# Small prologue loads moved from SyncE's to ScalarE's DMA queue in a two-block transformer kernel

## What is computed

```python
mod = jax.nn.silu(c) @ w_mod[l] + b_mod[l]
shift, scale, gate = jnp.split(mod, 3, axis=-1)
mod_c = jax.nn.silu(c_ctx) @ w_mod[l] + b_mod[l]
u = rms_norm(h, norm_w[l]) * (1.0 + scale[:, None, :]) + shift[:, None, :]
uc = rms_norm(hc, norm_w[l]) * (1.0 + scale_c) + shift_c
p = u @ w_in[l]
q, k, v = qk_heads(p, q_norm_w[l], k_norm_w[l])
q = rope_2d(q, angles)
```

## Time and profile before

| | us |
|---|---|
| median of 3 runs | 1993.04 (1991.38 to 1993.1) |
| profiled execution | 1991.96 |
| its span, first to last instruction | 1990.3 |
| PE busy | 1774.3 |
| DVE busy | 943.5 |
| ACT busy | 654.2 |
| POOL busy | 521.7 |
| mean DMA rate over the span | 94 GB/s |

### The profile page before, as it was taken

The page is one execution under the profiler, slowest core; times in us unless marked ns, Lnnn a source line. Parts: engine busy times, 40 slices in busy tenths (PEclk is TensorE's granted clock), DMA queues, the critical chain, the costliest instruction groups (busy, mean ns, idle before and its releaser), DMA issues.

```text
span 1990.3 us, 24899 instructions
## 1 busy us (share of the span) xinstructions
PE 1774.3 (89%) x10049; PEld 1484.2 (75%) x10049; DVE 943.5 (47%) x1232; ACT 654.2 (33%) x933; POOL 521.7 (26%) x441
## 2 busy tenths in 40 slices
PE   4997599778697789989999999899677999999997
PEld 3796499568695677668888777799566678888875
DVE  1568577675477764453333222533564343233223
ACT  4312255421223334242322212421564243333113
POOL 0005700344744000358878200078000000000000
PEclk8898799889898889999999999999878999999999
DMA  8453300134522000335556222222100212323321
GB/s 279 156 166 106 106 1 1 66 120 146 180 79 83 1 1 1 127 102 179 194 181 191 92 86 98 65 85 86 42 1 1 85 64 90 100 86 99 101 74 42
DMA packets 154445, 187.22 MB, mean 94 GB/s; under 512 B 6765, under 2 KB 121813, under 8 KB 154356
## 3 DMA queue, kind: packets, MB, share of 16 engines
q1 hardware_dynamic: 154356, 185.96, 29.0%
HBM read 183.85 MB, written 2.10 MB: 93 GB/s over the span
## 4 chain that ended last, share of the span: by engine, by line
PE 61%; POOL 15%; issue 8%; DVE 8%; ACT 5%; DMA 3%; POOLq 0%; SPq 0%; DVEq 0%; ACTq 0%
PE ps L694 7%; PE ps L695 7%; PE ps L696 7%; POOL msum L536 5%; POOL mraw L529 5%; PE ps L712 4%; PE ps L714 4%; PE ps L715 4%; PE ps L1044 4%; PE ps L1045 4%; PE ps L1046 4%; PE ps L788 2%; DMA mfirst<-in_w_mod_dram 1%; DMA mraw<-in_w_mod_dram 1%; PE ps L1017 1%
## 5 line engine op out<-in xcount | busy, mean ns | idle before, releaser
L1044 PE MATMUL ps<-uH,whi 128*128 128x512 f32 x704 | 277.6, 394 | 11.0 <-DVE uL L1581 11.0
L1565 DVE TENSOR_TENSOR wlo<-wraw,whi 128x2048 fp32r<-128x2048 f32 x71 | 176.5, 2487 | 218.8 <-ACT whi L1175 218.6
L1046 PE MATMUL ps<-uH,wlo 128*128 128x512 f32 x704 | 275.6, 392 | 0.0
L1045 PE MATMUL ps<-uL,whi 128*128 128x512 f32 x704 | 275.6, 391 | 0.0
L1175 ACT ACTIVATE whi<-wraw 128x2048 fp32r<-128x2048 f32 x71 | 135.7, 1911 | 346.8 <-PE ps L696 327.9
L712 PE MATMUL ps<-whi,uH 128*128 128x256 f32 (+1 forms) x800 | 230.8, 289 | 11.2 <-DVE uL L1581 11.2
L529 POOL TENSOR_TENSOR mraw<-mraw,cpad 128x1024 f32<-128x1024 f32 x64 | 128.4, 2007 | 398.9 <-PE ps L635 256.6
L714 PE MATMUL ps<-wlo,uH 128*128 128x256 f32 (+1 forms) x800 | 229.4, 287 | 0.0
L715 PE MATMUL ps<-whi,uL 128*128 128x256 f32 (+1 forms) x800 | 229.1, 286 | 0.0
L712 PEld LDWEIGHTS ps<-whi,uH 128*128 128x128 f32 x800 | 157.2, 196 | 12.8 <-issue 12.7
L1044 PEld LDWEIGHTS ps<-uH,whi 128*128 128x128 f32 x704 | 133.2, 189 | 41.1 <-issue 10.8
(11 more groups left out here) (389 smaller groups left out, 3200.6 us busy)
## 6 DMA issues: line engine op xcount, KB each, us to landing
mraw<-in_w_mod_dram SPq DMA_DIRECT2D x104, 512.0 KB, 3.9
wraw<-in_w_gate_dram SPq DMA_DIRECT2D x22, 1024.0 KB, 5.3
wraw<-in_w_up_dram SPq DMA_DIRECT2D x22, 1024.0 KB, 5.5
wraw<-in_w_down_dram SPq DMA_DIRECT2D x16, 1024.0 KB, 5.1
wraw<-in_w_in_odd_dram SPq DMA_DIRECT2D x12, 1024.0 KB, 5.1
wraw<-in_w_in_dram SPq DMA_DIRECT2D x11, 1024.0 KB, 5.4
wraw<-in_w_in_even_dram SPq DMA_DIRECT2D x9, 1024.0 KB, 6.5
mfirst<-in_w_mod_dram SPq DMA_DIRECT2D x16, 512.0 KB, 7.3
```

Source lines behind the costliest of these rows:

```text
L1044: mm(o, h_, uH[:, k], start=(k == 0), stop=False)
L1045: mm(o, h_, uL[:, k], start=False, stop=False)
L1046: last = mm(o, l_, uH[:, k], start=False, stop=(k == KT - 1))
L1565: V.tensor_tensor(wlo[:, n % 2, :], wraw[:, n % 2, :], whi[:, n % 2, :].bitcast(F32), ALU.subtract).then_inc(lo_done, 1)
```

## The change

The same 24 loads, with the same semaphores, are issued by ScalarE ahead of its first wait, in the same order (fifteen vectors, nine tables). SyncE's program begins with tick 0, and its tables between tick 15 and chunk 1 are gone. No load, no size and no wait is changed otherwise.

```diff
@@ SyncE
-            row = lambda ap: ap.rearrange("(r f) -> r f", f=P)
-            for r, ap in ((VC, t["c"][0]), (VCC, t["c_ctx"]), (VC2, t["c_2"][0]), (VBM, t["b_mod"][0]),
-                          (VNW, t["norm_w"][0]), (VCB, t["conv_b"][0]), (VLW, t["conv_ln_w"][0]),
-                          (VLB, t["conv_ln_b"][0]), (VBP, t["b_pw"][0])):
-                v = row(ap)
-                sp.dma_start(vr1[r:r + v.shape[0], 0], v).then_inc(vec_in, 16)
-            sp.dma_start(vr1[0:NV2, 1], t["b_mod_2"].rearrange("l (r f) -> (l r) f", f=P)).then_inc(vec_in, 16)
-            for r, name in ((0, "ln_mix_g_2"), (16, "ln_mix_b_2"), (32, "ln_ffn_g_2"), (48, "ln_ffn_b_2")):
-                sp.dma_start(vr1[r:r + 16, 2], t[name].rearrange("l (r f) -> (l r) f", f=P)).then_inc(vec_in, 16)
-            sp.dma_start(cwr[0:TAPS, :], t["conv_w"][0]).then_inc(vec_in, 16)
             for kp in range(4):
                 load_tick(0, kp)
...
                 if g == 3:
-                    sp.dma_start(ropet[:, 0], t["cos1"].rearrange("(t p) n -> p t n", p=P)).then_inc(tab_in, 16)
-                    sp.dma_start(ropet[:, 1], t["sin1"].rearrange("(t p) n -> p t n", p=P)).then_inc(tab_in, 16)
-                    sp.dma_start(qkw[:, 0], t["q_norm_w"].to_broadcast([P, HD])).then_inc(tab_in, 16)
-                    for tt in range(TT):
-                        sp.dma_start(posi[:, tt:tt + 1], t["positions_2"][0, tt * P:tt * P + P]
-                                     .rearrange("(p o) -> p o", o=1)).then_inc(tab_in, 16)
-                    sp.dma_start(ifr[:, :], t["inv2"].to_broadcast([P, 32])).then_inc(tab_in, 16)
-                    sp.dma_start(qkw[:, 1], t["k_norm_w"].to_broadcast([P, HD])).then_inc(tab_in, 16)
                     load_chunk(1)
@@ ScalarE, ahead of its first wait
+            row = lambda ap: ap.rearrange("(r f) -> r f", f=P)
+            for r, ap in ((VC, t["c"][0]), (VCC, t["c_ctx"]), (VC2, t["c_2"][0]), (VBM, t["b_mod"][0]),
...
+                act.dma_start(vr1[r:r + v.shape[0], 0], v).then_inc(vec_in, 16)
...
+            act.dma_start(cwr[0:TAPS, :], t["conv_w"][0]).then_inc(vec_in, 16)
+            act.dma_start(ropet[:, 0], t["cos1"].rearrange("(t p) n -> p t n", p=P)).then_inc(tab_in, 16)
...
+            act.dma_start(qkw[:, 1], t["k_norm_w"].to_broadcast([P, HD])).then_inc(tab_in, 16)
 
             act.wait_ge(vecT, 1)
             A(cols[:], X[:, 0, 0:NCOL], ACT.Copy).then_inc(cols_rd, 1)
```

More of the change, by code:

```diff
@@ L1161, in link @@
                 act.wait_ge(ach, n_[0])
+            row = lambda ap: ap.rearrange("(r f) -> r f", f=P)
+            for r, ap in ((VC, t["c"][0]), (VCC, t["c_ctx"]), (VC2, t["c_2"][0]), (VBM, t["b_mod"][0]),
+                          (VNW, t["norm_w"][0]), (VCB, t["conv_b"][0]), (VLW, t["conv_ln_w"][0]),
+                          (VLB, t["conv_ln_b"][0]), (VBP, t["b_pw"][0])):
+                v = row(ap)
+                act.dma_start(vr1[r:r + v.shape[0], 0], v).then_inc(vec_in, 16)
+            act.dma_start(vr1[0:NV2, 1], t["b_mod_2"].rearrange("l (r f) -> (l r) f", f=P)).then_inc(vec_in, 16)
+            for r, name in ((0, "ln_mix_g_2"), (16, "ln_mix_b_2"), (32, "ln_ffn_g_2"), (48, "ln_ffn_b_2")):
+                act.dma_start(vr1[r:r + 16, 2], t[name].rearrange("l (r f) -> (l r) f", f=P)).then_inc(vec_in, 16)
+            act.dma_start(cwr[0:TAPS, :], t["conv_w"][0]).then_inc(vec_in, 16)
+            act.dma_start(ropet[:, 0], t["cos1"].rearrange("(t p) n -> p t n", p=P)).then_inc(tab_in, 16)
+            act.dma_start(ropet[:, 1], t["sin1"].rearrange("(t p) n -> p t n", p=P)).then_inc(tab_in, 16)
+            act.dma_start(qkw[:, 0], t["q_norm_w"].to_broadcast([P, HD])).then_inc(tab_in, 16)
+            for tt in range(TT):
+                act.dma_start(posi[:, tt:tt + 1], t["positions_2"][0, tt * P:tt * P + P]
+                             .rearrange("(p o) -> p o", o=1)).then_inc(tab_in, 16)
+            act.dma_start(ifr[:, :], t["inv2"].to_broadcast([P, 32])).then_inc(tab_in, 16)
+            act.dma_start(qkw[:, 1], t["k_norm_w"].to_broadcast([P, HD])).then_inc(tab_in, 16)
             act.wait_ge(vecT, 1)
```

## The result

The changed kernel took 1999.82 us (median of 12 executions, 1995.05 to 2004.58); the kernel before, run beside it, 1992.11 (12 executions, 1991.07 to 1996.40). The ratio is 1.0034, 95% interval 1.0023 to 1.0046: slower by 4.6 to 9.2 us. A repeat of both gave 1.0027 (1.0013 to 1.0042), 2002.13 against 1996.59. The forecast was 1992.2, 0.8 us faster, with 1987.0 to 1996.5 around it, so it missed in sign and in range. The profiled execution of the changed kernel took 2004.19 us, its span 2002.5.

A forecast was written before the change was run, and what follows sets the result against it. TensorE was taken to bound the kernel, with loads binding only from 6.21 to 45.31 us; vectors at 16.1 bring the ninth weights from 34.21 to 33.4, so 1993.04 - 0.8 = 1992.2 us, range 1987.0 to 1996.5.

The forecast's parts named there:

- SyncE's start: Front of the kernel: first weights issued at about 0.8 us, DMA full from 2.5 to about 17, then a gap to about 22.
- conv_w on one engine, and its stretch: Last vector load: its 31 rows share one DMA engine, taking turns with the stream; 2.65 us of transfer plus 4.7 more.
- The start of conv_w at 7.9: Vector loads: conv_w begins at 7.9 us, after the weights' 5.4 us share of its engine and 0.6 for the small vectors.
- the formula: Front: the last weights move 1:1 with the vectors; gain is 17.0 minus their landing time, never over 5.7 us.
- rival 2: Vector loads land after the whole first 5 MB of the stream, at 19.5; 2.5 us slower, 1995.5 us; chance 0.18.
- From the vectors to the ninth issue: Front: cpad 3.69 us after the vectors, ticks 3.64, x tiles 5.38, issue 0.63 later; vectors at 16.1, ninth issue at 29.4.
- The ninth weights at latency, 3.9 us: Ninth weight load: lands 3.9 us after issue, at 33.4, since latency rules over rate (32.6); 0.8 us gained on 34.21.
- ScalarE free at 11.5: ScalarE's queue: the 24 issues take 10.7 us at SyncE's pace, hidden before its present wait for TensorE ends at 13.04.
- Rival 3: ScalarE's queue: slow issues, 1.06 us each, delay cols to 26.3 us; 2000.9 us, or 2007.6 at 1.34 each; chance 0.09.
- issues past 18 us: ScalarE's queue: its 24 issues done by 12 us; if they run past 18, the slow-issue case holds.
- Tables worth nothing: Nine table issues leaving SyncE's queue before chunk 1: chunk 1 issued some 5 us earlier, cost and gain zero.
- last weights to split constant: End of the front: last weights at 44.5 us, VectorE's split after 46.6 instead of 47.45, from there a constant shift.

The follow-up runs named there:

- e_after_split: The changed kernel with conv_w loaded in two pieces of 16 and 15 rows instead of one of 31; median 1997.87 us, ratio 1.0004 to the kernel before.
- r_after: The changed kernel run again unedited, for a second trace; median 2002.13 us, ratio 1.0027 to the kernel before.
- e_delay: The kernel before with one wait added, so SyncE's loads begin at 4.89 instead of 0.83 us; median 2001.44 us, ratio 1.0022.
- e_vec_act: The kernel before with only the fifteen vectors moved to ScalarE's queue, the nine tables left in SyncE's; median 1998.66 us, ratio 1.0010.
- e_after_angles: The changed kernel with VectorE's rotary angle operations moved into the attention loop, where GpSimd is idle; median 1999.08 us, ratio 1.0014 to the kernel before.
- e_angles: The kernel before with VectorE's rotary angle operations moved into the attention loop, where GpSimd is idle; median 1994.44 us, ratio 0.9994.

## Why the prediction was wrong, step by step

- **SyncE's start** at 0.8, DMA full from 2.5, then dry from 17 us: right (0.84; 378 GB/s; 42 GB/s from 17 us on). The gap lasted to 25.5 us instead of 22, for the tick was late.
- **conv_w on one engine, and its stretch**: right in mechanism and in size. Forecast were 2.65 + 4.7 = 7.35 us for its 31 rows; from the first start to the end of the last it took 7.1 (it met only 4 KB rows, no weights).
- **The start of conv_w at 7.9** is the step that failed. It started at 11.50. The sum charged the fourteen small loads ahead of it their own 0.6 us of engine time and no waiting, while it gave every row of conv_w a row of the stream to wait for. Their rows waited too, and more than row by row: by 8.0 us only 68 of their 232 rows of 512 bytes had started (all 232 by 6.98 in the kernel before), and the others then went beside x, about one for one. The last of them started at 11.30, right ahead of conv_w; with x held back conv_w started at 8.59. So conv_w began 3.6 us later than the sum has it, and 2.9 of that was waiting beside x.
- **The price of this**: vectors at 19.23 for 16.1. By the formula, 17.0 - 19.23, a loss of 2.2 us. It was rival 2's landing time that nearly came true (19.5), but not all of its mechanism. It had the whole of ScalarE's queue wait for the end of the 5 MB. Beside the weights the small rows were in fact held back (61 against 991); beside x they and conv_w took turns of one row, and conv_w came last because its 31 rows stood on one engine, behind the others. That the sum of the two is so near 19.5 is in part luck.
- **From the vectors to the ninth issue** forecast 13.3 us, measured 12.83: right.
- **The ninth weights at latency, 3.9 us**: wrong, a term mis-sized by 1.6. They took 5.47 from issue to use (37.53 - 32.06). In all kernels of the table it was 5.5 to 8.7, so 3.9 was never right behind weights 5 to 8 and chunk 0. The stream was full there (DMA share 0.98 from 25.5 to 37.5 us) at 344 GB/s and not at 386, which fits a ninth load that goes by the stream's rate. 2.2 + 1.6 less the 0.5 above gives 3.3, as measured at the ninth weights; at the last it was 3.5.
- **ScalarE free at 11.5**: wrong. Its last issue ended at 18.93. Fifteen vectors and two tables went at the expected pace; then one issue lasted 7.27 us. Here it cost nothing, since TensorE's transposes ended at about 20.6; with the vectors mended it does (e_after_split). Rival 3 was priced by an even pace for all 24, where the runs show one stall. The text's sign for it, issues past 18 us, came true without its cost: taken alone it would have misled.
- **Tables worth nothing, last weights to split constant**: right. 48.83 to 50.89 is 2.06; before, 45.31 to 47.37 by the same view. The tables were worth nothing in SyncE's queue; in ScalarE's they cost once the vectors were on time.
- **The range.** The front accounts for +3.5; 1993.04 + 3.5 = 1996.5, its very upper end. What is beyond is likely scatter: medians of the kernel before itself were 1992.11, 1996.59, 1996.53 and 1996.16. Its three times that were at hand (1991.38 to 1993.1) showed none of it, and the range allowed 1 us.

**Open** is what makes the stretch from 345 to 530 us last 178.6 to 181.9 us in four of the profiled executions and 184 to 187 in seven, among those of the kernels with the angles in their old place. The change isn't needed for it (the kernel before is in both groups), and it isn't the angles alone. But the four traces with a front more than 3 us late (changed, r_after, e_delay, e_vec_act) are all in the longer group, so that a late front makes the longer form more frequent is not excluded. That all of the first comparison's 7.7 us beyond the 3.3 to 4.2 of the front is this scatter is likely but not shown.

## What to carry to other kernels

When a load moves to a second queue beside a full stream, count its rows per DMA engine and let every one of them, those of all loads ahead too, wait for at least a row of the stream. A load whose rows all go over one engine, as the 31 here, comes last, so split it into counts that spread. Moving small loads out of the way of big ones helps only if their consumer isn't what frees the buffers of the big ones. And repeat the kernel before often enough to know its own scatter before a range of 0.2% is drawn.

## What the runs showed of the hardware beyond that

- A 62 KB load of 31 rows took 5.35 us from issue where it stood ahead of the stream in the same queue, and 12.6 (6.62 to 19.23) in a second queue beside a stream of 380 GB/s; split in 16 and 15 rows 5.8 from the second one's issue (7.18 to 12.98).
- An issue on ScalarE took 0.28 to 0.62 us for the fifteen vectors (0.28 to 0.43 on SyncE) and 0.40 for the cos table; sin took 0.78, and the next one 7.27 (7.30 in r_after, 7.33 in e_after_angles). With the tables left to SyncE there was no stall.
- VectorE operations of 128x128 took 0.23 to 0.29 us alone and 1.2 to 2.0 beside GpSimd's (in e_angles, with GpSimd idle, all sixteen 0.23 to 0.29), and which of them are hit differs between executions of one program.
